# Third layer's scan and stick-breaking start: where four groups of steps are issued, and two banks for the first q and k

## The reference, cut to what matters

```python
h = rmsnorm(x, norm_pre); proj = h @ w_in
z_ssd, xbc, dt_raw, q, k, v, z_sb, gates = split(proj)
xbc = silu(causal_conv4(xbc) + conv_b); xs, bm, cm = split(xbc)
dt = softplus(dt_raw + dt_bias); a = -exp(a_log)
# ssd_scan, per head and chunk
x_dt = xs * dt
decay = exp(segment sums of dt*a, causal); y_diag = ((cm @ bm^T) * decay) @ x_dt
states over chunks; y = y_diag + y_off + xs * d_skip
g = y * silu(z_ssd); y = g * rsqrt(mean(g*g) per group + eps) * ssd_norm     # two groups of 512
y_ssd = y @ w_ssd_proj
o = stick_breaking(q, k, v)       # sigmoids, cumulative products, 16 heads
y_sb = (o * silu(z_sb)) @ w_sb_proj
out = x + rmsnorm((sigmoid(g1) * y_ssd + sigmoid(g2) * y_sb) @ w_out, norm_post)
```

## Time and profile before

| what | value |
|---|---|
| median of three runs | 1274.64 us |
| the profiled execution's own time | 1276.48 us |
| its span, first to last instruction | 1274.7 us |
| mean granted TensorE clock | 0.997 |
| TensorE matmul busy | 1233.7 us, 97% |
| VectorE busy | 530.1 us, 42% |
| ScalarE busy | 579.5 us, 45% |
| GpSimd busy | 438.5 us, 34% |

### The profile page before, as it was taken

How to read it: one execution, slowest core, us unless ns; L and a number is a source line. 1 busy time by engine, 2 the same in 40 slices (tenths; PEclk the granted TensorE clock), 3 DMA queues, 4 the chain that set the end, 5 groups by cost and what they waited for, 6 DMA issues and landing times. The chain is left out here.

```text
span 1274.7 us, 16603 instructions
## 1 busy us (share of the span) xinstructions
PE 1233.7 (97%) x6339; PEld 947.7 (74%) x6339; DVE 530.1 (42%) x983; ACT 579.5 (45%) x1215; POOL 438.5 (34%) x241
## 2 busy tenths in 40 slices
PE   8999989999999999999899999999999999999998
PEld 7988745578988666678677777778666667878786
DVE  4211655634210455452466445420577771021343
ACT  6354655644333655453544323263555653332242
POOL 5534301213344222213244554343322323444451
PEclk9999989999999999999999999999999999999999
DMA  7433201202235999612223112223211112322331
GB/s 280 133 99 65 66 14 46 67 18 67 79 105 91 72 80 92 84 48 85 67 83 100 50 50 77 72 83 98 68 51 50 51 50 84 98 91 92 99 99 67
DMA packets 111311, 101.01 MB, mean 79 GB/s; under 512 B 22068, under 2 KB 97152, under 8 KB 111232
## 3 DMA queue, kind: packets, MB, share of 16 engines
q1 hardware_dynamic: 108688, 95.35, 31.8%
q0 software_dynamic: 864, 3.15, 0.7%
q10 hardware_dynamic: 1680, 1.44, 0.4%
HBM read 94.68 MB, written 2.10 MB: 76 GB/s over the span
## 5 line engine op out<-in xcount | busy, mean ns | idle before, releaser
L480 POOL TENSOR_TENSOR w_lo<-w_raw,w_hi 128x1024 fp32r<-128x1024 f32 (+4 forms) x172 | 391.7, 2278 | 769.5 <-ACT w_hi L475 769.5
L475 ACT ACTIVATE w_hi<-w_raw 128x1024 fp32r<-128x1024 f32 (+4 forms) x172 | 171.3, 996 | 279.5 <-PE bank L531 237.6
L531 PE MATMUL bank<-acts_hi,w_hi 128*128 128x512 f32 (+1 forms) x600 | 231.8, 386 | 6.4 <-POOL w_lo L480 4.7
L531 PE MATMUL bank<-acts_lo,w_hi 128*128 128x512 f32 (+1 forms) x600 | 230.2, 384 | 0.0
L531 PE MATMUL bank<-acts_hi,w_lo 128*128 128x512 f32 (+1 forms) x600 | 230.2, 384 | 0.0
L531 PEld LDWEIGHTS bank<-acts_hi,w_hi 128*128 128x128 f32 x600 | 112.0, 187 | 32.5 <-issue 5.2
L531 PEld LDWEIGHTS bank<-acts_lo,w_hi 128*128 128x128 f32 x600 | 112.0, 187 | 23.1
L531 PEld LDWEIGHTS bank<-acts_hi,w_lo 128*128 128x128 f32 x600 | 112.0, 187 | 22.3
L531 PE MATMUL bank<-w_hi,acts_hi 128*128 128x512 f32 (+3 forms) x324 | 114.2, 353 | 4.0 <-POOL w_lo L480 1.7
L531 PE MATMUL bank<-w_hi,acts_lo 128*128 128x512 f32 (+3 forms) x324 | 113.5, 350 | 0.0
L531 PE MATMUL bank<-w_lo,acts_hi 128*128 128x512 f32 (+3 forms) x324 | 113.5, 350 | 0.0
(11 more groups left out here) (255 smaller groups left out, 2032.8 us busy)
## 6 DMA issues: line engine op xcount, KB each, us to landing
w_raw<-in_w_in SPq DMA_DIRECT2D x68, 512.0 KB, 3.6
w_raw<-in_w_out SPq DMA_DIRECT2D x24, 512.0 KB, 3.5
w_raw<-in_w_in_b SPq DMA_DIRECT2D x22, 512.0 KB, 4.8
w_raw<-in_w_in_a SPq DMA_DIRECT2D x10, 512.0 KB, 3.8
w_raw<-in_w_mem_kv SPq DMA_DIRECT2D x8, 512.0 KB, 8.0
w_raw<-in_w_sb_proj SPq DMA_DIRECT2D x8, 512.0 KB, 3.4
w_raw<-in_w_ssd_proj SPq DMA_DIRECT2D x8, 512.0 KB, 3.5
w_raw<-in_w_in_b SPq DMA_DIRECT2D x8, 384.0 KB, 3.1
```

The lines of the kernel that those rows point to most:

```text
L475: nc.scalar.activation(w_at(p)[0][:, 0:size], w_raw[p % RAW][:, 0:size], ACT.Copy).then_inc(w_high.sem, 1)
L480: nc.gpsimd.tensor_tensor(lo[:, 0:size], w_raw[p % RAW][:, 0:size], hi[:, 0:size].bitcast(F32), ALU.subtract).then_inc(w_rest.sem, 1)
L531: mm = nc.tensor.matmul(bank_of(S, s, g)[0:lhs.shape[1], 0:rhs.shape[1]], lhs, rhs, start=j + kk + t == 0, stop=j == len(S.pieces) - 1 and ...
```

## The change

Six edits.

1. Silu: ScalarE's twelfth silu of the convolution is issued in the loop over f at f = 5 in place of f = 8.
2. Squares: ScalarE's four `norm_act_step` of the gated rows go from behind the last slot into it. Blocks 0 and 1 go behind the high part issued when piece 13 ends, blocks 2 and 3 behind the one issued when piece 14 ends.
3. Masks: GpSimd's `while` runs to `XT + 2 * (n - 1)`, so each rest is issued one mask later. The order becomes masks 0, 1, rest 0, masks 2, 3, rest 1, masks 4, 5, rest 2, masks 6, 7, 8, rest 3, masks 9, 10, rest 4, masks 11, 12, 13, rest 5, masks 14, 15, rest 6.
4. x times dt: VectorE's one instruction becomes four of 128 x 1024, each behind the two copies of its token block.
5. Banks: piece 1 of q and k goes to bank 1. It waits for nothing but its weights, and piece 2 waits for `qk` at 1.
6. Counts: 52 matmuls in place of 48 come before `score(0)`, and step s = 0 has 4 in place of 8 behind it.

```diff
@@ ssd_act
             for f in range(XT):
-                if f == 2 * MB:
+                if f == 5:
                     silu(S.n // 2 - 1, 3)
...
-            for m in range(MB):
-                norm_act_step(act, ssd_norm, m, lambda m: (sem["ssd_gated"], 2 * m + 2), rounds=False)
             project_act(act, pC_zs, between=lambda m: store_rows(act, m))
@@ beside_act
                 split_ahead_act(act, pC_z, 0, q)
+                for m in range(2 * (q - 13), 2 * (q - 13) + 2) if q in (13, 14) else ():
+                    norm_act_step(act, ssd_norm, m, lambda m: (sem["ssd_gated"], 2 * m + 2), rounds=False)
@@ ssd_pool
-                while n and done < XT + 2 * n:
+                while n and done < XT + 2 * (n - 1):
@@ ssd_dve
-            dve.wait_ge(sem["xT_out"], 2 * MB)
-            by_head = "p m (h d) -> p (m h) d"
-            link(nc.vector.tensor_tensor(c_xdt.rearrange(by_head, d=HD), c_x.rearrange(by_head, d=HD),
-                                         c_dt.rearrange("p m h -> p (m h)").unsqueeze(2).to_broadcast([P, MB * C_H, HD]),
-                                         ALU.mult))
+            for m in range(MB):
+                dve.wait_ge(sem["xT_out"], 2 * m + 2)
+                ins = nc.vector.tensor_tensor(c_xdt[:, m].rearrange("p (h d) -> p h d", d=HD),
+                                              c_x[:, m].rearrange("p (h d) -> p h d", d=HD),
+                                              c_dt[:, m].unsqueeze(2).to_broadcast([P, C_H, HD]), ALU.mult)
+            link(ins)
@@ stick_pe, stick_act
+        def qk_bank(q):
+            return bank[1 if q == 1 else 0]
...
-                        if q:
-                            pe.wait_ge(sem["qk"], q)
+                        if q > 1:
+                            pe.wait_ge(sem["qk"], q - (q == 2))
...
-                    mm = nc.tensor.matmul(bank[0][:, :], w[:, kk * P:(kk + 1) * P], acts[:, kk, :],
+                    mm = nc.tensor.matmul(qk_bank(q)[:, :], w[:, kk * P:(kk + 1) * P], acts[:, kk, :],
...
-            turn_in(48)
+            turn_in(48 + 4)
             for s in range(STEPS + 1):
                 score(s)
                 before, after = ((8, 6), (8, 2), (10, 6), (8, 0))[s % 4]
+                before -= 4 * (s == 0)
...
-                nc.scalar.activation((s_qT, s_kT)[q % 2][p % 2], bank[0][:, :], ACT.Copy,
+                nc.scalar.activation((s_qT, s_kT)[q % 2][p % 2], qk_bank(q)[:, :], ACT.Copy,
```

## The result

| | before | changed |
|---|---|---|
| median in the first comparison | 1274.64 us (5 runs) | 1265.11 us (5 runs) |
| lowest and highest | 1273.12, 1276.88 | 1265.03, 1269.08 |
| ratio of the two, 95% interval | | 0.9934 [0.9923, 0.9945] |
| span of the profiled execution | 1274.7 us | 1263.7 us |

The change is faster, by 0.55 to 0.77% with the interval. I had forecast 1266.8 us, that is 7.8 us or 0.61% less. The ratio forecast, 0.9939, lies inside the interval. The two profiled spans lie 11.0 us apart, also more than 7.8. Where both surpluses come from is the first thing to find.

A forecast was written before the change was run, and what follows sets the result against it. TensorE was taken as the bound, busy 1233.7 of 1274.7 us, so only its standstills could be won. Terms 1.83 + 0 + 2.75 + 2.07 + 1.14 = 7.79 us off 1274.64 gave 1266.8, range 1265.7 to 1270.3.

The forecast's parts named there:

- Silu: Convolution, step f = 8: TensorE's wait for the twelfth silu goes, 1.83 us saved, bounds 1.2 and 1.83.
- x times dt: VectorE's instruction in four parts: the GpSimd rest beside it ends earlier, but TensorE waits for neither; 0 us saved.
- Masks: Head loop: segment products 3, 5, 10 and 15 no longer wait for masks behind rests; 2.75 us saved with refills.
- Squares: Pieces 16 to 18: standstill of 2.31 before piece 18 goes, new one of 0.24 at piece 17; net 2.07 us saved.
- The chain of 3.61 us: Pieces 16 to 18: time from the start of ScalarE's high part to TensorE's start on that piece, 3.61 us.
- Banks and counts: Second q and k piece and first scores: 1.79 us gone, new standstill about 0.65 before second head's transposes; net 1.14.
- The median: Whole kernel: median 1274.64 us less 7.79 saved gives 1266.85, rounded 1266.8.
- B: Pieces 16 and 17: scaling of normed rows stretches each rest by 3.06 us; standstill 3.3 for 0.24, 1269.9 us; chance 0.10.
- C: First weights of the sweep: running products are slowed, bank edits bring -0.7 in place of 1.14, 1268.7 us; chance 0.07.
- D: Masks and high parts are late for reasons other than queue place; under 2.5 us saved, about 1273; chance 0.04.
- E: Piece 13: squares wait for late gated rows and hold high parts of pieces 16 and 17; slower, 1278.8 us; chance 0.03.

The follow-up runs named there:

- experiment 3: Changed kernel with squares one piece earlier and counts of steps 0 and 1 moved: 1266.37 and 1267.13 us; instead without the counts edit: 1267.64 us.

## Why the prediction was right, point by point

The mechanism came out: each standstill went with the edit that was to remove it, in the size forecast to 0.1 us, and the one edit forecast at nothing gave nothing. The level of the first median did not (see the point on the median). The order of the prediction's steps:

- **Silu**, forecast 1.83: 1.90 in the whole, 1.89 alone. ScalarE's idle time of 0.54 took it up, and the sixth copy follows at 700.68 without a wait for TensorE. The surplus of 0.07 is TensorE's refill behind the standstill, which I had counted for the masks and not here.
- **x times dt**, forecast 0: 0 alone. The rest beside it ended earlier, as forecast, but took 3.02 and not near 2.5, and the parts ended 11.25 us after the first L1462 in place of some 10.4. The step that was wrong is the length of a part, which I took as 1.1 throughout. The parts and GpSimd's masks slowed each other: the two masks went from 2.51 to 3.49, the four parts took 6.33 where the whole took 4.43, most of it in the two parts beside the masks (2.07 each against 1.21). So the last part still ran for 0.79 us beside the rest: it ended at 705.57, and 705.57 + 2.38 = 707.95 is near the rest's end at 707.80, as 713.39 and 713.23 were before. The Trainium skill (SBUF — State Buffer, Who interferes with whom) says that a VectorE instruction with two inputs in SBUF contends with a GpSimd instruction that reads SBUF, over a shared pair of ports that is an exclusive lock. By that rule both queues lengthen when they run side by side, and these rows agree.
- **Masks**, forecast 2.75: 2.64 between the first and last product and 0.11 behind it. Four standstills gone with their refills, none new.
- **Squares**, forecast 2.07: 2.11. The chain of 3.61 us met the start of piece 17 exactly. The squares began 0.1 us sooner than I had allowed and so the copies of v ended 0.1 sooner, and TensorE came 0.13 late and not 0.24. That the total agrees to 0.04 is partly luck: I had left TensorE's refills out here on both sides, 0.08 behind the old standstill and 0.1 or more behind the new one, and they about cancel. With the refill the new one cost 0.27 (experiment 3).
- **Banks and counts**, forecast 1.14: 1.19, with the new standstill of 0.6 where the forecast had 0.65. The counts' own share, 0.16, I had not split off. They trade one wait (0.85) for another of nearly the same size (0.6), so they were hardly worth an edit.
- **The median**, forecast 1266.8 with a range from 1265.7, measured 1265.11, which lies below the range, and 1266.49 in the repeat, inside it. The saving was right and the starting level was not. My sum was taken from the median of three runs of the kernel before, all from the middle of the three groups of its runs, and the middle group of the changed kernel, 1266.42 to 1266.75, lies right below the forecast. Four of the first five runs of the changed kernel fell into the lowest group and took the median there; whether a median of five does so is chance, and I had given it no term. I had read in the page a mean clock of 0.997 for a kernel that is at 1.00 in both windows that I gave, and had not asked where the missing 0.3% were. The two windows at 170 and 175 us hold 5 x 0.44 + 5 x 0.24 = 3.4 us of missing clock, 0.27% of the span: nearly all of it.
- **Rivals.** B (rests stretched by 3.06 us) did not come: 2.74 in place of 2.39 for piece 16, 2.40 for piece 17. C (slower running products) did not: the first two last 1.54 and 1.22 as before. Of D nothing shows: no segment product waits for a mask. Nor of E: the squares did not wait for the gated rows, since the first block starts 0.97 after the high part in front of it, ScalarE's own pace.

## What to carry to other kernels

Where one engine is the bound, look for each of its standstills and ask what the releasing instruction was itself waiting behind. If it stood in its own queue behind something with later data, moving it costs nothing, and such gains add up one by one. Give the place to which a step moves a chain length measured in the same trace, from the instruction held up to the start of the bound engine: one number (3.61 us) forecast when TensorE would start again to 0.1 us, and the same chain shows that a place one piece later loses more than the edit gains. Count TensorE's refill behind a standstill (about 0.1 us here) on both sides. Before crediting a change, compare the part of the trace that it can't touch. Here that part differed by 3 us. And before subtracting from a median of a few runs, see whether the runs fall into groups.

## What was not expected of the hardware

- In programs that are the same up to there the granted clock fell between 170 and 180 us in six traces (to 0.56 and then 0.76 in the kernel before) and stayed at 1.00 in six others, with the same two standstills (0.88 and 1.53 us) ahead of it; the kernel before and the changed one came out of it 3.0 us apart. With nine small matmuls in these standstills it was 1.00 in both traces, and there were no more runs 3 us and more above the lowest.
- Two parts of x times dt took 2.07 us beside two masks on GpSimd, the other two 1.21; a rest beside a VectorE instruction ended about its own 2.38 us after that instruction's end, whether it had run beside it for 3.22 us (5.44 in all) or for 0.79 (3.02).
- A standstill of 2.15 us on TensorE left the granted clock at 1.00 (kernel before, 850.70 to 853.00). One of 4.40 us was followed by matmuls 0.43 us apart in place of 0.23 for 3.7 us, which made it 1.6 us dearer.
